# Modulation sums spread over the stages of a two-block transformer kernel, its first norm worked k by k

## What is computed

```python
def adaln_norm(x, c, g, w_ada, b_ada):          # first block, twice
    mod = jax.nn.silu(c) @ w_ada + b_ada        # 1024 -> 3 x 1024
    shift, scale, gate = jnp.split(mod, 3, axis=-1)
    h = rms_norm(x, g) * (1.0 + scale[:, None, :]) + shift[:, None, :]
    return h, gate[:, None, :]

for i in range(DEPTH):                          # i = 0: nsa_mixer, i = 1: dilated_mixer
    h, gate = adaln_norm(x, c, norm_g[i], ada_w[i], ada_b[i])
    x = x + gate * mixer[i](h)
x = rms_norm(x, final_g)

mod = c_act @ ada_w_2 + ada_b_2                 # second block: 1024 -> 6 x 1024
shift1, scale1, gate1, shift2, scale2, gate2 = jnp.split(mod, N_MOD, axis=-1)
h = modulate(rmsnorm(x, norm1_g), shift1, scale1)
# window attention and a short convolution, then
x = x + gate1 * (merged @ w_out)
x = x + gate2 * peer(modulate(rmsnorm(x, norm2_g), shift2, scale2))   # experts
```

## Time and profile before

| | us |
|---|---|
| three executions | 2503.53, 2503.62, 2490.76; median 2503.53 |
| the profiled execution | 2499.82 |
| its span | 2497.7 |
| PE busy | 2274.4 (91%) |
| DVE busy | 1564.9 (63%) |
| ACT busy | 912.0 (37%) |
| POOL busy | 1308.2 (52%) |

### The profile page before, as it was taken

The page is one execution under the profiler, slowest core; times in us unless marked ns, Lnnn a source line. Parts: engine busy times, 40 slices in busy tenths (PEclk is TensorE's granted clock), DMA queues, the critical chain, the costliest instruction groups (busy, mean ns, idle before and its releaser), DMA issues. The chain is left out here.

```text
span 2497.7 us, 31948 instructions
## 1 busy us (share of the span) xinstructions
PE 2274.4 (91%) x11815; PEld 1968.0 (79%) x11815; DVE 1564.9 (63%) x2923; ACT 912.0 (37%) x1502; POOL 1308.2 (52%) x691
## 2 busy tenths in 40 slices
PE   2699699988999887968899999999999899999998
PEld 1588578776787775756789999999999788788776
DVE  6321587844522557364229999999995566667665
ACT  1212355423224532152323333355554333333332
POOL 0324011034542133312426888876665899999996
PEclk7799899988999988989899999999999999999999
DMA  6323064622221021101215888899998899999996
GB/s 234 135 85 109 16 216 153 216 75 71 84 85 34 26 68 59 68 26 43 85 66 179 290 288 276 273 336 353 338 335 306 321 336 354 344 343 339 355 335 231
DMA packets 164330, 492.40 MB, mean 197 GB/s; under 512 B 15056, under 2 KB 64464, under 8 KB 162768
## 3 DMA queue, kind: packets, MB, share of 16 engines
q1 hardware_dynamic: 107728, 305.79, 35.2%
q0 software_dynamic: 36864, 134.23, 14.7%
q10 hardware_dynamic: 19584, 50.34, 5.3%
HBM read 437.87 MB, written 52.43 MB: 196 GB/s over the span
## 5 line engine op out<-in xcount | busy, mean ns | idle before, releaser
L1996 POOL TENSOR_TENSOR t_split<-t_raw,t_split 128x1024 fp32r<-128x1024 f32 x256 | 631.2, 2466 | 148.7 <-ACT t_split L1923 145.3
L215 POOL TENSOR_TENSOR w_split<-ring,w_split 128x1024 fp32r<-128x1024 f32 x113 | 272.7, 2420 | 531.5 <-ACT w_split L207 531.4
L1889 PE MATMUL ps<-t_split,w_split 128*128 128x512 f32 x2304 | 532.5, 392 | 11.0 <-DVE w_split L2164 6.7
L1855 PE MATMUL ps<-h_hi,t_split 128*128 128x384 f32 x2048 | 536.6, 338 | 6.3 <-POOL t_split L1996 3.3
L1889 PEld LDWEIGHTS ps<-t_split,w_split 128*128 128x128 f32 x2304 | 432.0, 189 | 111.4 <-POOL t_split L1996 13.1
L237 PE MATMUL ps<-h_hi,w_split 128*128 128x512 f32 x1472 | 479.8, 403 | 14.3 <-POOL w_split L215 14.3
L1923 ACT ACTIVATE t_split<-t_raw 128x1024 fp32r<-128x1024 f32 x256 | 270.3, 1057 | 364.8 <-DMA t_raw<-v_table 222.7
L1855 PEld LDWEIGHTS ps<-h_hi,t_split 128*128 128x128 f32 x2048 | 373.1, 189 | 8.6 <-POOL t_split L1996 5.1
L237 PEld LDWEIGHTS ps<-h_hi,w_split 128*128 128x128 f32 x1472 | 279.8, 190 | 82.1 <-issue 15.6
L1855 PE MATMUL ps<-h_lo,t_split 128*128 128x384 f32 x1024 | 343.4, 335 | 0.0
L237 PE MATMUL ps<-h_lo,w_split 128*128 128x512 f32 x736 | 289.4, 393 | 0.0
(11 more groups left out here) (306 smaller groups left out, 3271.5 us busy)
## 6 DMA issues: line engine op xcount, KB each, us to landing
ring<-w_stream SPq DMA_DIRECT2D x219, 512.0 KB, 3.3
t_raw<-u_table SPq DMA_DIRECT2D x128, 512.0 KB, 4.8
t_raw<-v_table SPq DMA_DIRECT2D x128, 512.0 KB, 5.3
gelu_scratch<-e_gel ACTq DMA_DIRECT2D x128, 192.0 KB, 5.0
gates_scratch<-arena ACTq DMA_DIRECT2D x8, 3072.0 KB, 13.1
arena<-gelu_scratch SPq DMA_DIRECT2D x32, 768.0 KB, 5.6
arena<-gates_scratch SPq DMA_DIRECT2D x32, 768.0 KB, 8.8
xT<-x_in SPq DMA_DIRECT2D x2, 1024.0 KB, 11.7
```

The source lines that it names most:

```text
L215: pool.tensor_tensor(w_split[:, i % RS, 1, :], ring[:, n % R, :], w_split[:, i % RS, 0, :].bitcast(F32), ALU.subtract).then_inc(lo_done, 1)
L1855: mm = pe.matmul(ps[:, 6 + n % 2, 0:NT], t_split[:, n % RAWS, u, k * P:(k + 1) * P], h_parts[h][:, k, P:T], start=(k + u + h == 0), stop=( ...
L1889: mm = pe.matmul(ps[:, 2 * i + half, :], w_split[:, b % 2, w, at:at + P], t_split[:, m % RAWS, v, half * 512:(half + 1) * 512], start=(n + ...
L1996: pool.tensor_tensor(t_split[:, m % RAWS, 1, :], t_raw[:, m % RAWS, :], t_split[:, m % RAWS, 0, :].bitcast(F32), ALU.subtract).then_inc(t_ ...
```

## The change

1. **Opening.** n0 becomes a ColumnNorm that keeps all eight squares (`stored=True`): ACT squares, PE sums them in 32 one-column matmuls, DVE works the root (`dve_chain`) between its 12th and 13th piece, PE spreads it between chunks 0 and 1. Scaling and parts move to the next block, where units 0 and 1 are worked k by k and POOL waits until all eight k are done. `cmp_in` is loaded and split in the opening. Only 16 modulation pieces stay there. The first 256 columns of the constants load behind x, the others behind the 18th piece.
2. **Order of chunks.** The vectors are summed in the order MOD_ORDER: 0, 1, 2, 3, 11, then 4 to 10.
3. **First projection.** 24 pieces (chunks 2 to 4), in the stream between q, `cmp_w1`, `vsw` and z pieces. DVE sums ten behind rope 7, six behind rope 9, eight behind the small copies. PE works chunks 2 and 3 after the `vsw` units, chunk 4 before the last z unit. POOL works ropes 7 to 9 ahead of the splits of units 12 to 14.
4. **NSA attention.** 32 pieces (chunks 5 to 8), at a pace of 0.375 and 0.625 per unit of three and four blocks.
5. **Dilated projection.** 24 pieces (chunks 9 to 11). The sums of chunks 9 and 10 are kept in PSUM banks 6 and 7 (`ada_acc`); ACT copies each to SBUF for PE. Chunks 9 and 10 follow unit 20, chunk 11 unit 30.
6. `piece_used` counts no modulation pieces any more (`used_of`); `invf` moves to the small constants; bias and amps are added by chunk (`ada_take`).

The core of the diff:

```diff
+def stream():
...
+    load("ada", 12)
+    load("cmp_in", 2)
+    load("ada", 4)
+    load("ksw", 2)
+    load("q", 7)
+    load("ada")
+    load("q")
+    load("ada")
+    for _ in range(8):
+        load("cmp_w1")
+        load("ada")
+    for _ in range(3):
+        load("vsw")
+        load("ada", 2)
+    load("z")
+    for _ in range(4):
+        load("z")
+        load("ada", 2)
+    load("z", 3)
+    load("ada", 32)
+    load("nsa_out", 8)
+    for x in range(32):
+        load(("dq", "dk", "dv", "dz")[x // 8])
+        if 2 <= x < 18 or 22 <= x < 30:
+            load("ada")
...
+MOD_ORDER = (0, 1, 2, 3, 11, 4, 5, 6, 7, 8, 9, 10)
...
+            def act_squares_stored(self, act):
+                for k in range(KD):
+                    act.activation(self.sq[:, k, :], xT[:, k, :], ACT.Square).then_inc(self.squared.sem, 1)
...
-        n0 = norm_parts("n0", xT, ntmp, nsq, KD, 6, amp[:, 0, :], mod[:, 0:8], h_parts)
+        n0 = ColumnNorm(0, amp[:, 0, :], mod[:, 0:8], (5,), stored=True)
...
+                n0.pe_sums_stored(pe)
+                ada_chunk(pe, 0, ada_sum0, 6)
+                n0.pe_spread(pe)
+                ada_chunk(pe, 1, ada_sum0, 6)
...
-                for j in range(16):
-                    ada_piece(dve, j, ada_sum0, 0)
+                for j in range(KD + 4):
+                    ada_piece(dve, j, ada_sum0)
+                n0.dve_chain(dve)
+                for j in range(KD + 4, 2 * KD):
+                    ada_piece(dve, j, ada_sum0)
...
-                for u in range(12):
+                feature_group(pe, units2[0:2], (0, 1), h_parts, n0.done)
+                for u in range(2, 12):
...
+                ada_chunk(pe, 2, ada_sum0, 7)
+                ada_chunk(pe, 3, ada_sum0, 7)
...
-                for r in range(10):
+                for r in range(8):
                     rope_nsa[2](dve, r)
+                for j in range(2 * KD, 2 * KD + 10):
+                    ada_piece(dve, j, ada_sum0)
+                rope_nsa[2](dve, 8)
+                rope_nsa[2](dve, 9)
+                for j in range(2 * KD + 10, 4 * KD):
+                    ada_piece(dve, j, ada_sum0)
...
-        ada_pace, ada_after, due = (0, 0, 0.5, 0.75, 1.0), [], 0.0
+        NSA_ADA = 4 * KD
+        ada_pace, ada_after, due = (0, 0, 0, 0.375, 0.625), [], 0.0
...
+        ada_acc = ps[:, 6:8, :].rearrange("p a b -> p (a b)")
...
+                for j in range(9 * KD, 9 * KD + 2):
+                    ada_piece(dve, j, total=ada_acc)
                 for r in range(16):
+                    j = 9 * KD + 2 + r
+                    if j < 11 * KD:
+                        if j == 10 * KD:
+                            dve.wait_ge(ada_moved, 1)
+                        ada_piece(dve, j, total=ada_acc)
                     rope_dil[2](dve, r)
```

More of the change, by code:

```diff
@@ L170, in build @@
         split_of, n_split = {}, 0
-        for name, _ in STREAM:
-            for n in range(*PIECE_AT[name]):
-                if name not in RAW:
-                    split_of[n] = n_split
-                    n_split += 1
+        for n, name in enumerate(STREAM):
+            if name not in RAW:
+                split_of[n] = n_split
+                n_split += 1
         split_list = sorted(split_of)
@@ L268, in token_unit, with ada_piece @@
                     mm.then_inc(piece_used, 1)
-        def ada_piece(dve, j, sums, which):
-            piece, chunk, k = (ADA0[0] + j if j < 24 else ADA12[0] + j - 24), j // KD, j % KD
-            total, c = sums[:, chunk % 2, :], csil[:, which, k:k + 1]
+        def ada_piece(dve, j, sums=None, total=None):
+            piece, chunk, k = ada_list[j], j // KD, j % KD
+            which = int(MOD_ORDER[chunk] >= 6)
+            c = csil[:, which, k:k + 1]
             dve.wait_ge(piece_in[piece % R], 16 * (piece // R + 1))
+            if total is None:
+                total = sums[:, chunk % 2, :]
+                if k == 0 and chunk >= 2:
+                    dve.wait_ge(ada_taken, chunk - 1)
             if k == 0:
-                if chunk >= 2:
-                    dve.wait_ge(ada_taken, chunk - 1)
                 dve.tensor_scalar(total, ring[:, piece % R, :], c, None, ALU.mult).then_inc(ada_used, 1)
@@ L293, in ada_chunk, with ada_take @@
             mm.then_inc(ada_taken, 1)
+        mod_taken = sem("mod_taken")
+        Work.taken = 0
+        def ada_take(dve, chunk, bank):
+            dve.wait_ge(ada_taken, chunk + 1)
+            cols = slice(MOD_ORDER[chunk] * KD, (MOD_ORDER[chunk] + 1) * KD)
+            dve.tensor_tensor(mod[:, cols], ps[:, bank, cols], S("adab")[:, cols], ALU.add).then_inc(mod_taken, 1)
+            Work.taken += 1
         h_parts = (h_hi, h_lo)
@@ L464, in pe_sums, with pe_sums_stored @@
                                        C("ones")[:, 0:1], start=True, stop=True)
+                mm.then_inc(self.summed.sem, 1)
+            def act_squares_stored(self, act):
+                for k in range(KD):
+                    act.activation(self.sq[:, k, :], xT[:, k, :], ACT.Square).then_inc(self.squared.sem, 1)
+            def pe_sums_stored(self, pe):
+                self.squared.wait(pe, KD)
+                for i in range(TT):
+                    for k in range(KD):
+                        at = i if k < KD - 1 else 2 * TT + i
+                        mm = pe.matmul(ps[:, 7, at:at + 1], self.sq[:, k, tile_tokens(i)], C("ones")[:, 0:1],
+                                       start=(k == 0 or k == KD - 1), stop=(k >= KD - 2))
                 mm.then_inc(self.summed.sem, 1)
@@ L1276, in _ @@
                                     ps[:, 6 + v % 2, :].rearrange("p (a b) -> p a b", b=P)).then_inc(v_taken, 1)
+                for j in range(11 * KD + 4, 12 * KD):
+                    ada_piece(dve, j, ada_sum6)
+                ada_take(dve, 9, 4)
+                ada_take(dve, 10, 4)
+                ada_take(dve, 11, 5)
+                dve.wait_ge(mod_taken, Work.taken)
+                dve.scalar_tensor_tensor(out=amp[:, 3, :], in0=mod[:, 80:88], scalar=1.0, in1=S("n2g"),
+                                         op0=ALU.add, op1=ALU.mult)
         kd_pad = place("kd_pad", HR_AT, [2, KD, T])
@@ L2267, in constants @@
     put("sin", np.sin(angle))
-    put("invf", inv)
     u = np.arange(T)
@@ L2316, in small_arrays @@
     put("pev", x["nsa_pe_v"][0].reshape(16, P).T)
+    inv = np.float32(10000.0) ** (-np.arange(HALF, dtype=np.float32) / np.float32(HALF))
+    put("invf", inv.astype(np.float32)[np.arange(P) % HALF])
     put("w2k", x["nsa_ck_w2"][0].reshape(2, P, DH).transpose(1, 0, 2))
```

245 lines of the change are left out of this document (139 added, 106 removed).

## The result

The change makes the kernel slower: 2509.9 us in the median of 20 runs (2501.3 to 2519.6) against 2494.7 for the kernel before (20 runs, 2489.5 to 2506.9), ratio 1.0052 with a 95% interval of 1.0037 to 1.0067. I had forecast 2500 and no change. The profiled executions stand at 2497.7 us of span before and 2507.6 after, 9.9 apart; the medians are 15.2 apart, and the runs of one kernel differ by some 18.

A forecast was written before the change was run, and what follows sets the result against it. Opening taken as DMA-bound, first projection and NSA attention as PE-bound, with clock drops after PE waits. Terms -33.5 + 28.4 + 9.2 + 8.2 - 19 + 7.2 = +0.5 on 2499.8 gave 2500 us (chance 0.58); range 2470 to 2515.

The forecast's parts named there:

- Opening, -33.5: Up to the first units' copies: only 16 modulation pieces ahead, first projection matmul at 53.3 instead of 86.92; 33.5 us saved.
- Compression, +28.4: Compression matmuls: PE waits 3.9 us before the second `cmp_w1` piece, then seven pieces at half speed, 7.1 each; 28.4 us lost.
- Behind it, +9.2: After compression: value projection starts 8.6 us after instead of 1.4, 7.2 lost, plus 2 for first matmuls at low clock.
- chunks in the first projection, +8.2: Three chunks of 1.84 us move into the first projection, 5.5, plus 2.7 for two low-clock stretches; 8.2 us lost.
- NSA attention, -19: NSA attention: five fewer chunks 9.2, three low-clock stretches saved 5.0, idle PE won 4.8; 19 us saved.
- the bound of 24.7: Upper bound on the NSA attention saving: 9.2 + 8.3 + 7.2 = 24.7 us.
- The drain stays at half clock: End of NSA attention: last piece still due at the last unit, so the drain keeps 0.50 clock.
- Dilated projection, +7.2: Dilated projection: three chunks 5.5 and one low-clock stretch 1.7, its 24 sums free; 7.2 us lost.
- its rival: Dilated projection: DVE's sums collide with POOL's work, up to +20.5 us, total 2521 us; chance 0.15.
- First rival, the clock holds or comes back: Compression: clock stays at or returns to full, 23.5 us less than the sum, 2477 us; chance 0.27.

The follow-up runs named there:

- x4: Changed kernel with modulation pieces 16 to 18 summed after ropes 5 to 7 instead of after rope 7; 2480.8 us.
- x10: x2 with PE held ahead of the second `cmp_w1` piece until VectorE has done four idle sums behind rope 7; 2496.3 us.
- x6: Changed kernel with 16 idle 512-column matmuls behind the second `cmp_w1` piece; 2496.9 us.
- r_before: The kernel before, unchanged, run again for a second profile; 2494.4 us, one run.
- r_after: The changed kernel, nothing changed, run again for a second profile; 2505.0 us, one run.
- x11: Changed kernel with 30 idle one-column matmuls at the very start of PE's program; 2498.8 us, ratio to before 1.0028.
- x8: Kernel before with 34 idle one-column matmuls on PE in the opening; 2505.5 us, ratio to before 1.0038.
- x3: Changed kernel with chunk 4's 16 one-column matmuls two z units earlier; 2511.3 us, ratio 1.0059.
- x7: Changed kernel with 30 idle one-column matmuls on PE in the opening, behind the norm's sums; 2510.2 us.
- x2: New opening, three chunks in the dilated projection, one under z, six in NSA attention, no modulation among the compression pieces; 2473.9 us, ratio to the kernel before 0.9907.

## Why the prediction was wrong

Point by point, by its own steps.

- *Opening, -33.5:* -35.7. Right, the first matmul even 1.4 us earlier than 53.3. The ring covered DVE's stop for the square root: the second chunk starts at 44.79 (45.5 foreseen).
- *Compression, +28.4:* from 126.1 to 180.0 is 53.9 us, +25.4. The mechanism is shown by x4, x10 and x6. Off by size: wait 3.2 in place of 3.9, a piece 6.7 in place of 7.1. The Trainium skill ("TensorE: Matmul & The Clock Gate", Part 1) says that sustained PE activity releases the throttle. Here 47 us of nearly unbroken 62-column matmuls did not, and 16 wide ones did within 6 us (x6); the measurement decides. That narrow matmuls never bring the clock back is not shown either: in seven of the 16 profiles it came back within the drain of NSA attention, among matmuls of 64 and 128 columns.
- *Behind it, +9.2,* and *chunks in the first projection, +8.2:* the value projection starts 187.95 - 180.01 = 7.9 us after compression, before 1.4, so +6.5 of the 7.2; everything from there to compressed attention +9.7 where 2 and 8.2 were foreseen. Right together.
- *NSA attention, -19:* -25.2 in the first pair of profiles, just outside the bound of 24.7, but 219.4 and 199.7 us, -19.7, in the second (r_before, r_after). "The drain stays at half clock" holds in one profile of each kernel and fails in the other, so that step is neither right nor wrong: this stage varies by 2 to 3 us from one execution to the next, and the forecast lies within that.
- *Dilated projection, +7.2:* +8.2. Right, and its rival did not come.
- *First rival, the clock holds or comes back:* it did not; x4 shows what it would have given, 2481, nearly its 2477.

Of the whole, -1.2 us at 918 was measured (-3.2 in the second pair) and +0.5 foreseen. The step that failed is an unspoken one: the sum has no term for the part of the program that the diff doesn't touch, and so puts its change at nothing without a reason. Behind 918 us it lost 11 (14 in the second pair), and 8.5 of it at the change of the tables: because PE's program was of another length, one fetch of its instructions fell at the start of the gates' store and one among the gathers. Moving them away (x11) is worth 11 us of the median; what the change itself costs is then 1.0028, 4.7 us against before, within what I forecast as the same. With the fetches in the bad place in both, x8 and the changed kernel, the difference is about the same, 4.4 us. The 6.4 us of compressed attention are in the profiled execution, and by r_after not in every one.

That 2509.9 still lies inside the stated range, 2470 to 2515, is no merit of the mechanism: the base of the sum, 2499.8, was one execution, 5 us above the median of 20, and the range was wide enough for a loss that I had not thought of.

Open stays the stretch from 918 to the tables: 393.8 to 394.2 us in the eight profiles of kernels with the changed stream in the first projection (the changed kernel twice, x3 to x7 and x11), 390.0 to 390.6 in the eight others. The low stretches near 1062 and 1100 us are 6.8 and 17.1 us long in the changed kernel, 3.4 and 13.7 in the one before; 6.8 us more at half speed cost up to 3.4, an estimate, which would be nearly all of it. Why they are longer stays open. Neither PE's instruction count (x7, x8) nor the dilated chunks (x2) decide it. I did not find what does.

## What to carry to other kernels

Look for where a queue issued in order puts a transfer that is needed now behind one whose slot is freed by another engine later; ahead of narrow matmuls such a wait can cost not its own length but the clock for the stretch behind it, here 29 us for 3.2. A change of some ten us can also come from where a long program's instruction fetches fall: before explaining a loss in code that nothing touched, compare the fetches of the two traces, and shift the program by idle instructions in a place where their engine has nothing to do. Take a second profile of the unchanged kernels before a stage's 6 us is put down to an edit.

## What the hardware showed that I had not expected

- PE's instructions are fetched in pieces of some 16 KB through the DMA engines that carry the data, 14 to 33 us apart around the tables. Where one fell 0.4 to 4.4 us behind the issue of a 3 MB store, the store landed 11.0 to 12.8 us after its issue in place of 10.5 and SP's turn came after 17.2 to 19.1 in place of 16.0. With a second fetch among the gathers, the gap was 14.0 to 15.7 us in place of 6.5 to 7.0.
- 16 wide matmuls begun at 0.50 took 5.95 us, and the clock came back within them; it then held through 16 us of narrow ones (x6). A wait of only 0.82 us was followed by a fall there.
- The same kernel, executed twice, can keep the clock in a stage of narrow matmuls or lose it: 44.2 and 50.6 us for compressed attention in the changed kernel, and 2.8 or 5.2 us for the drain's last 24 matmuls in both kernels.
- A sum of a modulation piece with its total in PSUM takes 1.28 us beside POOL's splits, an add of two SBUF operands 2.42 where it is 0.69 alone. With the total in SBUF the sum took 1.56 in the mean of seven. The Trainium skill ("SBUF — State Buffer", the section "SBUF: two separate sides") says that a VectorE instruction with two SBUF inputs takes turns with a GpSimd one that reads SBUF, and names no such rule for one with its other input in PSUM; the trace agrees.
